# A differential attention in which each pair of score tiles waits for its own rotated tiles

## The chip, the cores and the metric

The kernel runs on one core of one Trainium2 chip. The metric is the device time of one execution in microseconds. Five engines work side by side: TensorE (PE) multiplies, VectorE (DVE), ScalarE (ACT) and GpSimd (POOL) do the rest, SyncE (SP) issues most transfers. They meet at semaphores.

## The reference

Two blocks are computed on 512 tokens of width 1024, in float32. The first has a recurrent unit, a sparse attention and a mixture of 32 experts. The second has two layers, and only these are touched. A layer projects its input to three attentions and their gates:

```
(na_q, na_k, na_v, df_q, df_k, df_v, m_cq, m_ckv, m_kr, gate_pre) = split(x @ w_in[l])
na_out  = neighbourhood_attention(...)          # 8 heads of 64
# differential attention, 4 heads, two score matrices each:
q1, q2, k1, k2 = rope(...)                      # first 16 of 64 dims rotated
o   = softmax(q1 k1) v - lam * softmax(q2 k2) v
df_out = rms_norm(o, subln_g) * (1 - lam_init)  # over the 128 values of a head
mla_out = latent_attention(m_cq, m_ckv, m_kr, ...)
merged = sum_i sigmoid(gate_i) * (out_i @ w_branch[i]);  x = layer_norm(a*x + merged @ w_out)
# then a gated feed-forward of width 2816 and a second layer_norm
```

## The kernel before

Everything is kept transposed: 128 features on the partitions, 512 tokens in the free dimension, so a "tile" is 128x512. Weights come in slots of 16 chunks (128x128 each, 1 MB a slot) through a ring of five slots. A product of full accuracy is made of three fast ones (`tile3`, L437 to L439): high part times high part, high times low, low times high. So each slot is split: ACT copies its high part (`weights_hi`, L486) into one of three high slots, and POOL subtracts (`weights_lo`, L496). A slot's high place comes free when PE begins the next slot (`said`, semaphore `w_used`). The order in which slots come is written in `stream_plan`, and every engine walks the same order by hand.

Products land in two double-buffered pairs of PSUM banks: A (banks 0 and 1, emptied by ACT) and B (banks 2 and 3, emptied by DVE). `claim` on PE waits until the bank before the last one is free; `take` waits until it is full.

Per layer, PE goes through these stages, and the change touches all but the first:

1. First attention (`units_pe`), with the tiles of its gate woven in.
2. `out_tile` of `na_o`: eight tiles of four chunk products each, of the attention's output. They read `o_hi` and `o_lo`, which DVE makes in `heads_split` (L1270, L1271) after the last head.
3. `values(df_v)` (L972 to L974): the values of the second attention, 96 matmuls, in three passes over two slots.
4. Eight tiles `df_qk` (four of queries, one per head, then four of keys). ACT copies each to `raw`, PE multiplies it by a permutation (`turn`, L993, bank B), DVE rotates it (`rope`, L1275 to L1278) and signals `roped`.
5. The pairs: 16 of them, (head, query block). In step i PE makes the two score tiles of pair i (L1012; banks 4 and 5 for even pairs, 2 and 3, which are B's, for odd ones), a part of a gate tile (`woven`, L727 to L729), the transposes of pair i-2 (L1021), and after a head's fourth pair its product with the values (L1028). DVE takes two maxima (L1308), ACT two exponents (L1164), DVE scales and joins them (`pair`, L1298 to L1301).
6. Latent projections: five tiles (`cq`, `mckv`) and a narrow one (`kr`), and between them the norm of the four heads. For head m: ACT squares it into `sqb` (L472), DVE copies it to `acc` (L542), PE sums over the partitions by four products with a column of ones (`squares_pe`, L448), DVE and ACT take the inverse root (L552 to L565), PE spreads it over the partitions (`spread_pe`, L457) after the next tile, DVE copies the spread from PSUM to `acc` (L568) and scales the head (L1319). The next head's copy L542 stands behind that in DVE's order, since both use `acc`.
7. Tiles of the second attention's output, which read its own high and low parts, mixed with more gates; then the third attention.

Of the kernel before, what the change touches and what calls it, by code (L numbers as in the profile page):

```python
# [8 lines left out]
P = 128  # L9
SEQ = 512  # L10
D = 1024
DC = D // P
NQB = SEQ // P
# [68 lines left out]
def stream_plan():  # L82

    gates = [(f"mg{m}", CHUNKS) for m in range(MG_SLOTS)]
    first = [("xr", RC * DC), ("rg", 2 * RC), ("ckv", KVC * DC), ("qi", 4 * DC), ("ki", DC),
             ("wi", 1), ("gr", RC * DC)] + gates + [("q", HEADS * DC),
             ("uk", HEADS * KVC), ("uv", 4 * 2 * KVC), ("rnn_out", DC * RC), ("att_out", DC * DC),
             ("out", DC * DC), ("router", 3)]
    layer = [("na_v", 4 * DC), ("na_qk", 8 * DC), ("na_g", DC * DC), ("na_o", 4 * DC),
             ("df_v", 4 * DC), ("df_qk", 8 * DC), ("df_g", DC * DC), ("cq", MQC * DC), ("mckv", KVC * DC), ("kr", DC)]  # L90
    layer += [(f"df_o{n}", 4) if kind == "o" else (f"ml_g{n}", DC) for step in MIXED for kind, n in step]
    layer += [("qb", HEADS * MQC), ("kvb_k", 4 * KVC), ("kvb_v", 4 * KVC), ("ml_g", (DC - EARLY) * DC), ("ml_o", 4 * DC),
             ("out2", DC * DC), ("ffn_in", 2 * FFC * DC), ("ffn_out", DC * FFC)]

    blocks = {"uv": 16, "na_v": 16, "df_v": 16, "qb": 16, "kvb_v": 8, "ml_g": 16, "rg": 16, "ckv": 16, "gr": 16, "mg0": 16,
              "rnn_out": 16, "att_out": 16, "router": 16}

    def place(parts, at):
        found = {}
        for name, n in parts:  # L100
            if name in blocks:
                at += -at % blocks[name]
            found[name] = at
            at += n
        return found, at + -at % CHUNKS

    one, end = place(first, 0)
    two, size = place(layer, 0)
    return one, end, two, size
# [49 lines left out]
def build(nc, xT, crow, wmod, wrest, wfirst, wlayers, consts, vectors, brow, frow, lamv, rpb, w13, w2, out):  # L159
# [16 lines left out]
    with ExitStack() as ctx:  # L176
# [4 lines left out]
        def sem(name):  # L181
            return ctx.enter_context(nc.semaphore(name))
# [185 lines left out]
            "h1_turned", "h1_kept", "row_in", "h2_rdy", "v_mean", "v_squared", "v_scale", "v_rdy", "v_rest_rdy", "v_turned", "x_rdy"))  # L368
        lam_in, lam_sum, lam_exp = (sem(n) for n in ("lam_in", "lam_sum", "lam_exp"))
        rp_in, near_rdy, roped, keys_rdy = (sem(n) for n in ("rp_in", "near_rdy", "roped", "keys_rdy"))  # L370
        pair_exp, pair_norm, pair_turned, pair_pt = (sem(n) for n in ("pair_exp", "pair_norm", "pair_turned", "pair_pt"))
        pair_sc, pair_mx, o_rdy, merged_rdy = (sem(n) for n in ("pair_sc", "pair_mx", "o_rdy", "merged_rdy"))
        dev_rdy, dev_sq, dev_sq_in, norm_sums, norm_products, out_rdy = (sem(n) for n in (
# [360 lines left out]
        def units_pe(pe, units, ready, Pb=Pb, fill=None):  # L734

            U = len(units)
            for i in range(U + 3):
                if i < U:
                    u = units[i]
                    k = cnt["pv"] + i  # L740
                    ready(i)
                    if k >= 2:
                        pe.wait_ge(exp_done, k - 1)
                    ins = pe.matmul(ps[:, 4 + k % 2, 0:u["nk"] * P], u["q"], u["k"], start=True, stop=True)  # L744
                    ins.then_inc(sc_rdy, 1)
                if fill is not None:
                    fill(i)
                if 2 <= i < U + 2:
                    u = units[i - 2]
                    k = cnt["pv"] + i - 2  # L750
                    if u["summed"]:
                        pe.wait_ge(exp_done, k + 1)
                    else:
                        cnt["scaled"] += 1
                        pe.wait_ge(p_norm, cnt["scaled"])
                    if k >= 2:
                        pe.wait_ge(pt_rdy, k - 1)
                    for j in range(u["nk"]):
                        ins = pe.transpose(ps[:, 6 + k % 2, j * P:(j + 1) * P], Pb[:, k % 3, j * P:(j + 1) * P], ident)  # L759
                    ins.then_inc(turned, 1)  # L760
                if i >= 3 and "sum" in units[i - 3]:
                    pe.wait_ge(pt_rdy, cnt["pv"] + i - 2)
                    units[i - 3]["sum"](pe)
            cnt["pv"] += U
# [182 lines left out]
        def layer_pe(pe, l):  # L947
# [33 lines left out]
                tile3(pe, A.claim(pe), base["na_qk"] + m * DC, *xa, DC).then_inc(A.full, 1)  # L981
            assert B.made == B2 + l * B_LAYER, (B.made, B2)
            units_pe(pe, na_units(), lambda i: pe.wait_ge(A.free, A.made) if i == 0 else None, P2, woven(pe, base["na_g"], xa, DC, 3, 4))
            for m in range(DC):
                out_tile(base["na_o"] + 4 * m, 0, m)


            values(base["df_v"])

            def turn(perm, m, n=P):  # L990

# [5 lines left out]
                if m >= 1:  # L997
                    turn(K("perm_d"), A.made - 1)
            turn(K("perm_d"), A.made)
            pe.wait_ge(B.free, B.made)  # L1000
            pe.wait_ge(roped, l * 16 + 8)
            U = len(pairs)
            fill = woven(pe, base["df_g"], xa, DC, 1, 2)
            for i in range(U + 3):
                if i < U:
                    h, qb = pairs[i]
                    k = l * U + i
                    if k >= 2:
                        pe.wait_ge(pair_exp, 2 * (k - 1))
                    for a in range(2):  # L1010
                        r = 64 * a
                        pe.matmul(ps[:, pair_banks[k % 2][a], :], qk2[r:r + 64, h, qb * P:(qb + 1) * P], qk2[r:r + 64, 4 + h, :],  # L1012
                                  start=True, stop=True).then_inc(pair_sc, 1)
                fill(i)
                if 2 <= i < U + 2:
                    k = l * U + i - 2
                    pe.wait_ge(pair_norm, k + 1)
                    if k >= 2:
                        pe.wait_ge(pair_pt, k - 1)
                    for j in range(NQB):  # L1020
                        ins = pe.transpose(ps[:, 6 + k % 2, j * P:(j + 1) * P], P2[:, 2 * (k % 2), j * P:(j + 1) * P], ident)  # L1021
                    ins.then_inc(pair_turned, 1)
                if i >= 3 and pairs[i - 3][1] == NQB - 1:
                    h = pairs[i - 3][0]
                    pe.wait_ge(pair_pt, l * U + i - 2)
                    b = A.claim(pe)
                    for j in range(NQB):
                        ins = pe.matmul(b, v2[:, j, h * P:(h + 1) * P], PT2s[h % 2][:, j, :], start=(j == 0), stop=(j == NQB - 1))  # L1028
                    ins.then_inc(A.full, 1)

            for m in range(MQC + KVC):
                tile3(pe, A.claim(pe), base["cq"] + m * DC, *xa, DC).then_inc(A.full, 1)
                if m >= 1:
                    spread_pe(pe)
                if m < 4:
                    squares_pe(pe, 1)
            tile3(pe, A.claim(pe)[0:MLA_QK, :], base["kr"], *xa, DC, MLA_QK).then_inc(A.full, 1)
            kr_copied = A.made

# [63 lines left out]
        def layer_act(act, l):  # L1103
# [17 lines left out]

            def df_gates(i):

                if 2 <= i <= 16 and i % 2 == 0:
                    gate(df_gate[:, i // 2 - 1, :], 1, i // 2 - 1)

            def ml_gates(i):
# [14 lines left out]
                copy(qk2[:, m, :])  # L1142

            units_act(act, na_units(), None, P2, PT2s, gates=na_gates, between=na_weights, pv_before=B2 + l * B_LAYER)
            for m in (0, 4):
                weights_hi(act, base["na_o"] + 4 * m)

            for s_ in range(NQB):
                weights_hi(act, end1 + l * size2 + two["df_v"] + (CHUNKS if s_ == NQB - 1 else 0))
                copy(v2[:, s_, :])  # L1150
            for m in range(8):
                weights_hi(act, end1 + l * size2 + two["df_qk"] + m * DC)
                if m >= 2:
                    act.wait_ge(roped, l * 16 + m - 1)
                copy(raw[:, m % 2, :])
# [20 lines left out]
                if i % 4 == 2:  # L1176
                    weights_hi(act, base["df_g"] + (i // 4) * CHUNKS)
            act.wait_ge(A.free, A.took)
            squares(act, o2[:, 0:1, :], 1)
            for h in range(4):  # L1180
                if h + 1 < 4:
                    squares(act, o2[:, h + 1:h + 2, :], 1)
                weights_hi(act, end1 + l * size2 + two["cq"] + h * DC)
                copy(cq[:, h, :] if h < MQC else ckv2[:, h - MQC, :])
                root(act)
# [55 lines left out]
        def layer_dve(dve, l):  # L1241
# [70 lines left out]
            pair(U - 1)  # L1312
            a += 4 + DC
            for h in range(4):
                if h >= 1:
                    dve.wait_ge(o_rdy, 4 * l + h)
                sum_squares(dve, 1)
                inverse_var(dve, P, EPS)
                STT(out=o2[:, h, :], in0=o2[:, h, :], scalar=subg[:, l:l + 1], in1=rstd, op0=ALU.mult, op1=ALU.mult).then_inc(o_rdy, 1)  # L1319
            dve.wait_ge(A.free, a)  # L1320
            a += MQC + KVC + 1 + EARLY
            dve.wait_ge(o_rdy, 4 * (l + 1))
# [1283 lines left out]
```

## Time and profile before

| | |
|---|---|
| median of 3 runs | 3422.34 us (3411.9, 3422.34, 3423.8) |
| profiled execution | 3408.22 us, of which span 3406.1 us |
| PE busy in the span | 3062.2 us, 90% |
| DVE, ACT, POOL busy | 1547.6, 988.7, 941.6 us |
| chain that ended last, by engine | PE 74%, DMA 12%, DVE 9%, ACT 3% |
| mean granted clock of PE | 0.969 of 2.4 GHz |
| stages 2 to 6, layer 0 | 1395 to 1640 us of the span |
| stages 2 to 6, layer 1 | 2477 to 2728 us |

The profile is one execution. A line of the trace has the start, the busy time, the engine, the line of the kernel, what is written and read, and in brackets how long the engine had been idle and what ended that. A granted clock of 1.00 is 2.4 GHz, one of 0.50 is 1.2 GHz; a window between shows a mixture.

### The profile page before, as it was taken

The numbers are of one execution on the slowest core, as the hardware profiler recorded it, in microseconds if no ns is written. First come the engines' busy times: TensorE is split into PE (matmuls) and PEld (weight loads), VectorE is DVE, ScalarE is ACT, GpSimd is POOL, SyncE is SP. The second block draws the span as 40 slices with busy tenths as digits, with TensorE's granted clock in tenths as the row PEclk, the third lists the DMA queues.
The fourth block names the chain that finished last, engine by engine and source line by source line (L and its number), as shares of the span: only waits on it lengthen the run. The fifth ranks groups of instructions, "written<-read, shape, count | busy, mean of one in ns | idle before, by whom it ended". The sixth has DMA issues, their size and how long they took to land.

```text
span 3406.1 us, 32962 instructions
## 1 busy us (share of the span) xinstructions
PE 3062.2 (90%) x13112; PEld 2096.4 (62%) x13112; DVE 1547.6 (45%) x2578; ACT 988.7 (29%) x1398; POOL 941.6 (28%) x346
## 2 busy tenths in 40 slices
PE   3999998787777679999998899999999899889998
PEld 2777656632222256766655788877776665578886
DVE  7598866421111135455557622231636365752233
ACT  3553232200000043234253322223424334232222
POOL 2243102200000044322121444445432221244432
PEclk9999999899999989999999899999999899989999
DMA  5236212499999941211211222222121121112221
GB/s 225 85 124 237 98 50 87 167 400 422 422 422 422 384 145 62 75 62 50 77 48 39 73 99 99 99 87 94 49 87 50 50 83 42 50 63 98 99 99 50
DMA packets 71228, 465.80 MB, mean 137 GB/s; under 512 B 8784, under 2 KB 9072, under 8 KB 18992
## 3 DMA queue, kind: packets, MB, share of 16 engines
q1 hardware_dynamic: 60192, 436.31, 33.4%
q0 software_dynamic: 5200, 17.07, 1.4%
q10 hardware_dynamic: 5696, 10.49, 0.8%
q8 instruction: 95, 1.56, 0.2%
q14 instruction: 45, 0.37, 0.0%
HBM read 451.24 MB, written 12.60 MB: 136 GB/s over the span
## 4 chain that ended last, share of the span: by engine, by line
PE 74%; DMA 12%; DVE 9%; ACT 3%; issue 1%; POOL 0%; SPq 0%; ACTq 0%; DVEq 0%; POOLq 0%
PE ps L437 15%; PE ps L439 14%; PE ps L438 14%; DMA mring<-w 10%; PE ps L744 3%; PE ps L727 3%; PE ps L729 2%; PE ps L728 2%; PE ps L426 2%; PE ps L2248 2%; PE ps L907 1%; PE ps L759 1%; PE ps L1012 1%; PE ps L2323 1%; PE ps L1028 1%
## 5 line engine op out<-in xcount | busy, mean ns | idle before, releaser
L496 POOL TENSOR_TENSOR w_lo<-wring,w_hi 128x2048 fp32r<-128x2048 f32 (+1 forms) x198 | 812.6, 4111 | 1776.6 <-ACT w_hi L486 1776.5
L437 PE MATMUL ps<-x_hi,w_hi 128*128 128x512 f32 (+1 forms) x1480 | 593.0, 401 | 18.2 <-ACT ps L1585 7.8
L439 PE MATMUL ps<-x_hi,w_lo 128*128 128x512 f32 (+1 forms) x1480 | 582.7, 394 | 0.0
L486 ACT ACTIVATE w_hi<-wring 128x2048 fp32r<-128x2048 f32 x176 | 336.0, 1911 | 322.0 <-PE ps L437 284.7
L438 PE MATMUL ps<-xf_lo,w_hi 128*128 128x512 f32 x1080 | 422.2, 391 | 0.0
L437 PEld LDWEIGHTS ps<-x_hi,w_hi 128*128 128x128 f32 (+1 forms) x1480 | 281.8, 190 | 91.3 <-issue 8.4
L439 PEld LDWEIGHTS ps<-x_hi,w_lo 128*128 128x128 f32 (+1 forms) x1480 | 281.3, 190 | 60.7
L2322 PE MATMUL ps<-mring,xT__95 128*64 128x512 f32 x512 | 239.9, 600 | 58.3 <-DMA mring<-w 54.5
L2323 PE MATMUL ps<-mring,xT__95 128*64 128x512 f32 x512 | 240.2, 601 | 0.0
L438 PEld LDWEIGHTS ps<-xf_lo,w_hi 128*128 128x128 f32 x1080 | 204.1, 189 | 41.6
L1360 DVE TENSOR_TENSOR g_f<-ps,g_f 128x512 f32<-128x512 f32 x44 | 30.4, 692 | 366.7 <-PE ps L439 350.4
L2322 PEld LDWEIGHTS ps<-mring,xT__95 128*64 128x64 f32 x512 | 63.5, 136 | 185.7 <-DMA mring<-w 123.8
L438 PE MATMUL ps<-xa_lo,w_hi 128*128 128x512 f32 (+1 forms) x400 | 160.6, 401 | 0.0
L727 PE MATMUL ps<-x_hi,w_hi 128*128 128x512 f32 x336 | 159.2, 474 | 0.0
L2341 PE MATMUL ps<-mring,hidT 128*64 128x512 f32 x512 | 117.7, 602 | 42.4 <-DVE hidT L2080 42.4
L1692 ACT ACTIVATE sil<-ps 64x512 f32<-64x512 f32 x32 | 19.0, 595 | 471.1 <-PE ps L2323 471.1
L2075 DVE TENSOR_TENSOR hid<-ps,sil 64x512 f32<-64x512 f32 x32 | 21.8, 683 | 293.5 <-ACT sil L1692 293.5
L1476 POOL DMA_INDIRECT xs<-u_rows,ids x16 | 15.2, 951 | 461.9 <-PE ps L2311 405.5
L437 PE MATMUL ps<-g_hi,w_hi 128*128 128x512 f32 x352 | 137.7, 391 | 0.0
L439 PE MATMUL ps<-g_hi,w_lo 128*128 128x512 f32 x352 | 137.0, 389 | 0.0
L438 PE MATMUL ps<-g_lo,w_hi 128*128 128x512 f32 x352 | 137.0, 389 | 0.0
L729 PE MATMUL ps<-x_hi,w_lo 128*128 128x512 f32 x336 | 133.1, 396 | 0.0
(518 smaller groups left out, 5488.2 us busy)
## 6 DMA issues: line engine op xcount, KB each, us to landing
mring<-w SPq DMA_DIRECT2D x192, 1024.0 KB, 28.3
wring<-wlayers SPq DMA_DIRECT2D x148, 1024.0 KB, 4.8
wring<-wfirst SPq DMA_DIRECT2D x44, 1024.0 KB, 4.8
mods<-wrest SPq DMA_DIRECT2D x16, 1024.0 KB, 4.7
wmodS<-wmod SPq DMA_DIRECT2D x4, 2048.0 KB, 18.4
y_rows<-ysb ACTq DMA_DIRECT2D x64, 128.0 KB, 6.7
rp<-rpb POOLq DMA_DIRECT2D x16, 192.0 KB, 2.6
hT<-xT SPq DMA_DIRECT2D x1, 2048.0 KB, 18.2
```

The source lines that it names most:

```text
L426: ins = pe.matmul(bank, w[:, 0:m], rhs[:, k, :], start=(k == 0), stop=(k == nk - 1))
L437: said(pe.matmul(bank, wh[:, 0:m], hi[:, k, :], start=(k == 0), stop=False))
L438: pe.matmul(bank, wh[:, 0:m], lo[:, k, :], start=False, stop=False)
L439: ins = pe.matmul(bank, wl[:, 0:m], hi[:, k, :], start=False, stop=(k == nk - 1))
L486: act.activation(w_hi[:, q % HI_SLOTS, :], wring[:, home(g), :], ACT.Copy).then_inc(hi_rdy, 1)
L496: ins = pool.tensor_tensor(w_lo[:, home(slot), o:o + n], wring[:, home(slot), o:o + n], w_hi[:, q % HI_SLOTS, o:o + n].bitcast(F32), ALU.s ...
L727: said(pe.matmul(state["bank"], wh, x[0][:, k, :], start=(k == 0), stop=False))
L729: ins = pe.matmul(state["bank"], wl, x[0][:, k, :], start=False, stop=(k == DC - 1))
L744: ins = pe.matmul(ps[:, 4 + k % 2, 0:u["nk"] * P], u["q"], u["k"], start=True, stop=True)
L2322: pe.matmul(ps[MOE_ROWS:P, 2 + a, :], x, w[:, 0:SEQ], start=(k == 0), stop=(k == DC - 1))
L2323: ins = pe.matmul(ps[0:MOE_ROWS, 2 + a, :], x, w[:, SEQ:D], start=(k == 0), stop=(k == DC - 1))
L2341: ins = pe.matmul(ps[n * MOE_ROWS:(n + 1) * MOE_ROWS, 5 + a, :], hidT[:, a, k, :], w[:, n * SEQ:(n + 1) * SEQ], start=(k == 0), stop=(k == 3))
```

## The change

Four edits, in both layers of the second block:

- In the weights' order, on PE and on ACT, `df_v` comes ahead of `na_o`. DVE's order stays as it was.
- PE no longer waits for all eight rotated tiles before the pairs. The first pair of head h waits for `roped` up to key tile h (tiles 0 to 4+h), and pair 1 for the last turned tile to be out of bank B.
- The gate products are woven in quarters of a tile (6 matmuls): one each in steps 0, 1, 16 and 17, two in steps 2 to 15. Before it was a half (12 matmuls) in steps 1 to 16. ACT takes the last gate in step 17 and not in step 16.
- In the heads' norm PE sums straight from `sqb`, where ACT puts the squares, and DVE scales the head by the spread in PSUM. L542 and L568 are gone for the heads.

```diff
-    layer = [..., ("na_g", DC * DC), ("na_o", 4 * DC),
-             ("df_v", 4 * DC), ("df_qk", 8 * DC), ...
+    layer = [..., ("na_g", DC * DC), ("df_v", 4 * DC),
+             ("na_o", 4 * DC), ("df_qk", 8 * DC), ...
...
+            values(base["df_v"])
             for m in range(DC):
                 out_tile(base["na_o"] + 4 * m, 0, m)
-            values(base["df_v"])
...
-            pe.wait_ge(B.free, B.made)
-            pe.wait_ge(roped, l * 16 + 8)
             U = len(pairs)
-            fill = woven(pe, base["df_g"], xa, DC, 1, 2)
+            fill = woven(pe, base["df_g"], xa, DC, 0, 4)
+            pieces = [1, 1] + [2] * (U - 2) + [1, 1]
             for i in range(U + 3):
                 if i < U:
                     h, qb = pairs[i]
                     k = l * U + i
+                    if qb == 0:
+                        pe.wait_ge(roped, l * 16 + 4 + h + 1)
+                    if i == 1:
+                        pe.wait_ge(B.free, B.made)
...
-                fill(i)
+                for n in range(sum(pieces[:i]), sum(pieces[:i + 1])):
+                    fill(n)
...
                 if m < 4:
-                    squares_pe(pe, 1)
+                    pe.wait_ge(head_squared, 4 * l + m + 1)
+                    b = B.claim(pe)
+                    for s in range(NQB):
+                        ins = pe.matmul(b[:, s:s + 1], sqb[:, m % 2, s * P:(s + 1) * P], ones[:, 0:1], ...)
+                    ins.then_inc(B.full, 1)
...
-                if 2 <= i <= 16 and i % 2 == 0:
+                if 2 <= i <= 14 and i % 2 == 0 or i == 17:
                     gate(df_gate[:, i // 2 - 1, :], 1, i // 2 - 1)
...
-            for m in (0, 4):
-                weights_hi(act, base["na_o"] + 4 * m)
             for s_ in range(NQB):
                 weights_hi(act, ... two["df_v"] ...)
                 copy(v2[:, s_, :])
+            for m in (0, 4):
+                weights_hi(act, base["na_o"] + 4 * m)
...
-            squares(act, o2[:, 0:1, :], 1)
+            act.wait_ge(sq_added, cnt["sq_a"])
+            def head_square(h):
+                act.activation(sqb[:, h % 2, :], o2[:, h, :], ACT.Square).then_inc(head_squared, 1)
+            head_square(0)
             for h in range(4):
                 if h + 1 < 4:
-                    squares(act, o2[:, h + 1:h + 2, :], 1)
+                    head_square(h + 1)
...
             for h in range(4):
-                if h >= 1:
-                    dve.wait_ge(o_rdy, 4 * l + h)
-                sum_squares(dve, 1)
-                inverse_var(dve, P, EPS)
-                STT(out=o2[:, h, :], in0=o2[:, h, :], scalar=subg[:, l:l + 1], in1=rstd, ...)
+                inverse_root(dve, P, EPS)
+                STT(out=o2[:, h, :], in0=o2[:, h, :], scalar=subg[:, l:l + 1], in1=B.take(dve), ...)
+                free_bank_b(dve)
```

## Rows read from the trace of the kernel before

**Rows 1.** Page, part 1: busy time, share of the span, instructions.

```profile
PE 3062.2 (90%) x13112; PEld 2096.4 (62%) x13112; DVE 1547.6 (45%) x2578; ACT 988.7 (29%) x1398; POOL 941.6 (28%) x346
```

**Rows 2.** Windows, both layers: length, busy PE PEld DVE ACT POOL, granted clock, DMA.

```profile
1395.00:1640.00 245.00, 229.40 (x968) 166.49 (x967) 107.67 (x214) 80.85 (x134) 72.74 (x27) 0.97 0.19 65
2477.00:2728.00 251.00, 235.65 (x962) 170.67 (x962) 107.16 (x213) 80.52 (x133) 72.48 (x27) 0.94 0.18 63
```

**Rows 3.** Waits of PE, layer 0: waiting line, releaser: total us, times, longest.

```profile
PE ps L448 <- DVE acc L542: 8.0, 4, 2.0
PE ps L1012 <- DVE qk L1278: 2.7, 1, 2.7
PE ps L437 <- DVE o_lo L1271: 2.1, 1, 2.1
```

**Rows 4.** Timeline, first attention's end, both layers: start, us, instruction, [idle before].

```profile
1397.77 0.47 PE L437 MATMUL ps<-o_hi,w_hi 128*128 128x512 f32 x1 [2.13 <-DVE o_lo L1271]
...
1401.68 0.39 PE L437 MATMUL ps<-o_hi,w_hi 128*128 128x512 f32 x1
...
2479.14 0.75 PE L437 MATMUL ps<-o_hi,w_hi 128*128 128x512 f32 x1 [2.13 <-DVE o_lo L1271]
...
2483.56 0.39 PE L437 MATMUL ps<-o_hi,w_hi 128*128 128x512 f32 x1
```

**Rows 5.** Timeline at the start of the pairs, layer 0.

```profile
1491.76 2.03 PE L993 MATMUL ps<-raw,cs 128*128 128x512 f32 x4
1496.50 3.47 PE L1012 MATMUL ps<-qk 64*128 64x512 f32 x8 [2.71 <-DVE qk L1278]
...
1498.58 0.69 DVE L1308 TENSOR_REDUCE small<-ps 128x1 f32<-128x512 f32 x1 [2.23 <-PE ps L1012]
...
1500.28 0.69 ACT L1164 ACTIVATE P<-ps,small 128x512 f32<-128x512 f32 x1
...
1503.90 0.50 PE L727 MATMUL ps<-x_hi,w_hi 128*128 128x512 f32 x1
...
1506.78 0.60 PE L1021 MATMUL ps<-cs,P 128*128 128x128 f32 x4
1507.31 1.13 PE L1012 MATMUL ps<-qk 64*128 64x512 f32 x4
1508.37 0.50 PE L727 MATMUL ps<-x_hi,w_hi 128*128 128x512 f32 x1
```

**Rows 6.** Timeline at the last pair, layer 0.

```profile
1571.29 1.13 PE L1012 MATMUL ps<-qk 64*128 64x512 f32 x4
...
1580.89 0.66 PE L1021 MATMUL ps<-cs,P 128*128 128x128 f32 x4 [1.80 <-DVE P L1301]
```

**Rows 7.** Timeline of PE in the latent projections, layers 0 and 1.

```profile
1585.37 0.79 PE L437 MATMUL ps<-x_hi,w_hi 128*128 128x512 f32 x1
...
1601.42 1.05 PE L457 MATMUL ps<-cs,small 128*128 128x128 f32 x8
1604.51 1.13 PE L448 MATMUL ps<-cs,acc 128*128 128x1 f32 x8 [2.03 <-DVE acc L542]
...
1634.10 0.48 PE L437 MATMUL ps<-x_hi,w_hi 128*96 128x512 f32 x1
...
2670.34 0.80 PE L437 MATMUL ps<-x_hi,w_hi 128*128 128x512 f32 x1
...
2722.35 0.48 PE L437 MATMUL ps<-x_hi,w_hi 128*96 128x512 f32 x1
```

**Rows 8.** Windows around two of the falls of the clock, columns as in 2.

```profile
1604.00:1610.00 6.00, 5.49 (x21) 4.60 (x22) 1.43 (x7) 2.52 (x3) 1.24 (x1) 0.72 0.46 147
...
2700.00:2708.00 8.00, 7.33 (x22) 6.08 (x23) 1.58 (x8) 0.21 (x1) 0.00 (x0) 0.57 0.00 0
```

**Rows 9.** Page, part 5: splitting a weight slot into high and low parts.

```profile
L496 POOL TENSOR_TENSOR w_lo<-wring,w_hi 128x2048 fp32r<-128x2048 f32 (+1 forms) x198 | 812.6, 4111 | 1776.6 <-ACT w_hi L486 1776.5
...
L486 ACT ACTIVATE w_hi<-wring 128x2048 fp32r<-128x2048 f32 x176 | 336.0, 1911 | 322.0 <-PE ps L437 284.7
```

More of the change, by code:

```diff
@@ L88, in stream_plan @@
              ("out", DC * DC), ("router", 3)]
-    layer = [("na_v", 4 * DC), ("na_qk", 8 * DC), ("na_g", DC * DC), ("na_o", 4 * DC),
-             ("df_v", 4 * DC), ("df_qk", 8 * DC), ("df_g", DC * DC), ("cq", MQC * DC), ("mckv", KVC * DC), ("kr", DC)]
+    layer = [("na_v", 4 * DC), ("na_qk", 8 * DC), ("na_g", DC * DC), ("df_v", 4 * DC),
+             ("na_o", 4 * DC), ("df_qk", 8 * DC), ("df_g", DC * DC), ("cq", MQC * DC), ("mckv", KVC * DC), ("kr", DC)]
     layer += [(f"df_o{n}", 4) if kind == "o" else (f"ml_g{n}", DC) for step in MIXED for kind, n in step]
@@ L370, in build @@
         rp_in, near_rdy, roped, keys_rdy = (sem(n) for n in ("rp_in", "near_rdy", "roped", "keys_rdy"))
+        head_squared = sem("head_squared")
         pair_exp, pair_norm, pair_turned, pair_pt = (sem(n) for n in ("pair_exp", "pair_norm", "pair_turned", "pair_pt"))
@@ L1035, in layer_pe @@
                 if m < 4:
-                    squares_pe(pe, 1)
+                    pe.wait_ge(head_squared, 4 * l + m + 1)
+                    b = B.claim(pe)
+                    for s in range(NQB):
+                        ins = pe.matmul(b[:, s:s + 1], sqb[:, m % 2, s * P:(s + 1) * P], ones[:, 0:1], start=True, stop=True)
+                    ins.then_inc(B.full, 1)
             tile3(pe, A.claim(pe)[0:MLA_QK, :], base["kr"], *xa, DC, MLA_QK).then_inc(A.full, 1)
@@ L1314, in layer_dve @@
             for h in range(4):
-                if h >= 1:
-                    dve.wait_ge(o_rdy, 4 * l + h)
-                sum_squares(dve, 1)
-                inverse_var(dve, P, EPS)
-                STT(out=o2[:, h, :], in0=o2[:, h, :], scalar=subg[:, l:l + 1], in1=rstd, op0=ALU.mult, op1=ALU.mult).then_inc(o_rdy, 1)
+                inverse_root(dve, P, EPS)
+                STT(out=o2[:, h, :], in0=o2[:, h, :], scalar=subg[:, l:l + 1], in1=B.take(dve), op0=ALU.mult, op1=ALU.mult).then_inc(o_rdy, 1)
+                free_bank_b(dve)
             dve.wait_ge(A.free, a)
```

## The prediction

> **What bounds the kernel now.** I read the page first: PE is busy for 90% of the span [rows 1], so a change pays only where PE stands still, or where it runs at half clock. Then the windows over the stretch from the end of the first attention to the second attention's output, once per layer. The same work takes some 245 us in layer 0 and 251 us in layer 1; PE is busy for about 94% of both, and its mean clock is 0.97 and 0.94 [rows 2]. Hence about 15.5 us idle in each, and about 245 x 0.03 = 7 and 251 x 0.06 = 15 us of clock lost. DMA stands at 0.19 and POOL under a third, so neither weights nor their splitting set the pace.
>
> Third the waits of PE in layer 0, to see what ends the idle time [rows 3]. Three entries belong to the change: 8.0 us in four waits for DVE's copy of the squares, 2.7 us for the last rotated tile, 2.1 us for the first low part. Layer 1 has the same ones within 0.05 us.
>
> Last the clock, by small windows. Eleven windows hold all of its falls in the two stretches. A fall costs the whole of 6.0 x (1 - 0.72) = 1.7 us where it is single, and 8.0 x (1 - 0.57) = 3.4 us where it is double [rows 8]. In layer 0 one fall stands at the pairs' start and three in the latent projections, 6.8 us. In layer 1 one at the first attention's end, one at the pairs' start, a double one at the pairs' end, and in the projections a double one and three single ones: 15.3 us. Each begins behind one of the waits above, or while one lasts.
>
> **Edit 1, values first.** In layer 0 the first output tile begins after 2.13 us idle, and its four chunks then follow DVE's low parts: from 1397.77 to 1401.68 is 3.91 us [rows 4], where twelve matmuls at an undisturbed pitch take 2.75 us (rows 5 have it: 12 in 1503.90 to 1506.78 is 2.88, of which some 0.1 is the change of kind). With the values first, DVE splits the heads while PE works for over 20 us on operands that are there, so 2.13 + 1.2 = 3.3 us go. Layer 1: 2.13 + (2483.56 - 2479.14 - 2.75) = 3.8 us, its clock loss included [rows 4]. Sum 7.1 us.
>
> What is moved with it are the splits of slots. The values read their two slots in three passes and hold the first until 2.7 us before their end, so two of three high places stay taken. The output's first slot goes into the third place at once. Its second slot can be split only from then on: 1.9 us on ACT and 4.1 us on POOL [rows 9], 6.0 us, and it is needed 2.7 + 16 x 0.68 = 13.6 us later. The splits cost nothing as long as this cover of 7.6 us holds; the third rival takes it away. POOL's split now meets `heads_split` on DVE; both have more than 15 us to spare.
>
> **Edit 2, the pairs' start.** Before: turns from 1491.76, scores at 1496.50 after 2.71 us idle and partly at half clock, first transposes at 1506.78 [rows 5]. After: the turns end at about 1493.7, head 0 needs only key tile 4, done long before, so pair 0's scores run until 1494.8 (1.06 each, from 1507.31 to 1508.37) and a quarter of gate (1.5) until 1496.2. By then DVE has read the last turned tile, about 0.8 us ahead of the 1496.50 at which the rotation was known to be ready, so pair 1 goes on to 1497.3 and the second quarter to 1498.8. Step 2 needs pair 0's two exponents. DVE's maxima still stand behind its last rotation, so they begin at about 1496.4 instead of 1498.58; the second exponent began 1.70 us after that and takes 0.9 with its sum [rows 5], so PE is let on at 1499.0: 0.2 us of idle is left of 2.71. Scores and half a tile of gates bring the transposes to 1503.0. Pair 0's weights are ready at about 1496.4 + 2 x 1.70 + 1.6 = 1501.4. From there both kernels have the same work behind them. The gain is 1506.78 - 1503.0 = 3.8 us, of which 1.7 are clock. Twice, 7.6 us. Bounds: 2.1 us each if the clock falls anyway.
>
> **Edit 3, quarters.** The same 192 matmuls; slot limits fall at the same steps (5, 9, 13). Four more changes of kind at about 0.1 us. At the end I count no gain: pair 15's transposes start 1580.89 - 1571.29 = 9.6 us after its scores start, released by DVE [rows 6]. The new order has in that time 1.06 of scores, 2.88 + 1.5 + 1.5 of gates and two transposes of 0.53, 8.0 us; so PE still waits for DVE and ends at the same place, only in smaller waits. Bound above: the 1.80 of idle, twice. Bound below: if DVE were earlier, the last quarter could hold the transposes up by 1.5 us, twice.
>
> **Edit 4, squares from ACT's place.** The chain spread, copy L568, scale L1319, copy L542, squares is cut to spread, squares. In layer 0 the five tiles with their norms take 1634.10 - 1585.37 = 48.7 us, in layer 1 2722.35 - 2670.34 = 52.0 [rows 7]. Less the idle 8.0 [rows 3] and the clock loss of 5.1 and 8.5 (above) both give 35.5 us: the two layers agree on what the work takes alone. Nothing new should hold it: head m's squares lie ready a tile ahead (ACT makes them before the copy of tile m), the inverse root needs about 1.5 us and the spread comes 5.5 us later, and DVE frees the bank of the spread with the scaling, under 1 us. The gain is 13.2 + 16.5 = 29.7 us; without the clock 16.1.
>
> **Sum.** 7.1 + 7.6 + 29.7 = 44.4 us if no fall of the clock takes the place of a removed one. I charge 4 us, two or three single falls over the eight joints of spread and squares, where 2.1 us of small matmuls (1.05 each, [rows 7]) now follow each other. That gives 40 us: 3368 us for the profiled execution of 3408.22. The median of the runs shown is 14.1 us above that execution; what it holds more is not in this trace, and I leave it in. **3422.3 - 40 = 3382 us.**
>
> The spread multiplies by the identity, as a transpose does, and no row separates how such matmuls count for the clock. The Trainium skill, page TensorE: Matmul & The Clock Gate, Part 4: PE-mode transpose, states that transposes do not count as work in this way; here, with transposes in every step of the pairs, no window of them shows a low clock behind the first step, though gates fill these. By that rule the joints would stay slack for the clock, and the first rival would be likelier.
>
> **Rivals.** First, the clock falls all the same. For it: the falls come beside stretches with little matmul work, and spread plus squares are such. Against: the joint shrinks from 1.05 + 2.03 + 1.05 = 4.1 us [rows 7] to 2.1, and even at 4.1 one of eight stayed at full clock. Gain by idle alone: 2 x (2.13 + 1.2) + 2 x 2.1 + 16.1 = 27 us, so 3395 us. Chance 0.13.
>
> Second, a wait takes the place of the one removed at the pairs' start or in the norms, so that the change does only part of what it says. DVE still does its eight rotations before any maximum, and ACT's `root` stands behind a copy and, for heads 2 and 3, a split. If the pairs' start gave nothing and each of the later three joints kept 1.5 us, the gain would be 44.4 - 7.6 - 9 - 4 = 24 us, 3398 us; with the clock as in the first rival some 10, 3412 us. Against: the margins above, 4 us at each spread. Chance 0.10, of which 0.06 within 0.5%.
>
> Third, the other side: splits come late. If a slot of `na_o` or `df_qk` is not split when PE arrives, PE stands with all behind it. Cover is 7.6 us; a whole slot's delay beyond it costs 6.0 us and a fall of the clock, 1.7 [rows 8], and up to four slots per layer could be hit: 2 x 4 x 7.7 = 62 us against 40, 3444 us. It decides from 7.6 us lateness on. Against: POOL is busy a third of the stretch and DMA a fifth [rows 2]. Chance 0.03, and about half of it would be slower by over 0.5%.
>
> Fourth, more than I say: the pairs' end gives its 1.80 twice and the double fall there is gone (3.4): 44.4 + 7 = 51 us, 3371 us. Chance 0.10. The forecast itself has 0.64.
>
> **Range.** 0.5%, 17 us, is about what a measurement of this kernel can tell from no change; the three runs shown lie 12 us apart. Low end: 3371 less 9 of such scatter, 3362. High end: 3395 and 6 of scatter, 3401; that leaves out the worst of the second rival and the third. Faster by over 0.5%: 0.64 + 0.13 + 0.10 + 0.04 = 0.91; within: 0.06 + 0.01, 0.07; slower 0.02.
>
> **What would show it.** Right: the values' first matmul follows the last L885 without idle time, and the first output tile has an even pitch; scores of pair 0 right after the turns, a wait for ACT of under 0.5 us in step 2, the first transposes about 11.2 us after the turns' start and not 15.0; no wait before the squares' sums, L542 and L568 gone from the stage, and first `cq` tile to `kr` in about 35.5 to 39 us. Wrong: waits of PE on the exponents in steps 2 to 4, a clock of 0.50 at more than half of the norm's joints, or waits on the first matmul of a slot.

## The result, and the profile after

| | before | after |
|---|---|---|
| median | 3421.46 us (4 runs, 3411.9 to 3423.8) | 3365.55 us (4 runs, 3363.76 to 3368.4) |
| ratio | | 0.9839, 95% interval 0.9825 to 0.9853 |
| profiled execution | 3408.22 us | 3363.76 us |
| mean clock in it | 0.969 | 0.973 |

The kernel became 56 us faster, 1.6%. The forecast was 40 us and 3382 us, with a range from 3362 to 3401. The two profiled executions lie 44.5 us apart, and the sum before its charge for the clock was 44.4 us. That they agree so well is luck: the two stretches that the change touches became 48.8 us shorter, and the rest of the span, which it doesn't touch, came out 4.7 us longer in the changed kernel's profile (2911.1 and 2915.8 us). The experiments ask where the other 11 us of the medians come from, and whether each term is what it was said to be.

First the page of the changed kernel, busy time by engine. PE has 17 us less of busy time than in [rows 1] for the same 13112 matmuls: matmuls at half clock are longer ones.

```profile
PE 3045.0 (91%) x13112; PEld 2082.9 (62%) x13112; DVE 1536.4 (46%) x2562; ACT 988.9 (29%) x1398; POOL 942.7 (28%) x346
```

Then the windows of the two stretches, from the first attention's last product to the second attention's output (length, busy PE, PEld, DVE, ACT, POOL, clock, DMA share, GB/s). They answer to [rows 2]. They were 245 and 251 us long there; now both are 223.7 (223.1 from mark to mark, as the stretches are measured below), with the clock at 1.00 and 2.3 us idle in place of 15.5.

```profile
1397.80:1621.50 223.70, 221.40 (x967) 161.86 (x966) 101.92 (x206) 80.66 (x133) 72.78 (x27) 1.00 0.20 71
2460.80:2684.50 223.70, 221.40 (x967) 161.81 (x965) 101.93 (x206) 80.56 (x133) 72.77 (x27) 1.00 0.20 71
```

The waits of PE in the first stretch answer to [rows 3]. All three entries are gone. What stands instead is small: two waits for the weights of the last two pairs and one for the last transposed tile, as before.

```profile
PE ps L1024 <- DVE P L1311: 1.6, 2, 1.2
PE ps L1031 <- ACT PT2b L1177: 0.7, 1, 0.7
```

At the end of the first attention [rows 4] the values start right behind the last product, with no idle time in brackets, and the output's chunks run at an even 0.68 us from the first on:

```profile
1396.01 2.40 PE L886 MATMUL ps<-PT2b,v 128*64 128x128 f32 x20
1398.34 0.50 PE L973 MATMUL ps<-w_hi,x_hi 128*128 128x512 f32 x1
...
1420.53 0.39 PE L438 MATMUL ps<-o_hi,w_hi 128*128 128x512 f32 x1
...
1421.20 0.39 PE L438 MATMUL ps<-o_hi,w_hi 128*128 128x512 f32 x1
...
1421.88 0.39 PE L438 MATMUL ps<-o_hi,w_hi 128*128 128x512 f32 x1
```

At the start of the pairs [rows 5] the turns begin at 1491.25, scores of pairs 0, 1 and 2 follow at 1493.21, 1495.85 and 1498.50 with a quarter of gate between them, none of them after a recorded wait. The first transposes come 11.17 us after the turns' start; the forecast was 11.2, before it was 15.02:

```profile
1491.25 2.03 PE L992 MATMUL ps<-raw,cs 128*128 128x512 f32 x4
1493.21 1.13 PE L1014 MATMUL ps<-qk 64*128 64x512 f32 x4
...
1495.85 1.13 PE L1014 MATMUL ps<-qk 64*128 64x512 f32 x4
...
1498.50 1.13 PE L1014 MATMUL ps<-qk 64*128 64x512 f32 x4
...
1502.42 0.60 PE L1024 MATMUL ps<-cs,P 128*128 128x128 f32 x4
```

At the last pair [rows 6] the 1.80 us have split in two, 1.18 and 0.42: together 1.6 us, which is what the prediction's 9.6 us less 8.0 leave. The last transposes start 1576.53 - 1566.93 = 9.6 us after the scores, as before. The product with the values still waits its 0.69, and POOL's split (5.64 us) still runs beside DVE's scaling of pair 14 (1.65 us here, 0.75 undisturbed):

```profile
1566.93 1.13 PE L1014 MATMUL ps<-qk 64*128 64x512 f32 x4
...
1569.51 5.64 POOL L497 TENSOR_TENSOR w_lo<-wring,w_hi 128x512 fp32r<-128x512 f32 x4 [15.70 <-ACT w_hi L487]
...
1572.36 1.65 DVE L1311 SCALAR_TENSOR_TENSOR P<-P,small 128x512 f32<-128x512 f32 x1
...
1574.07 0.66 PE L1024 MATMUL ps<-cs,P 128*128 128x128 f32 x4 [1.18 <-DVE P L1311]
...
1576.53 0.65 PE L1024 MATMUL ps<-cs,P 128*128 128x128 f32 x4 [0.42 <-DVE P L1311]
...
1577.87 3.70 PE L1031 MATMUL ps<-PT2b,v 128*128 128x512 f32 x8 [0.69 <-ACT PT2b L1177]
```

In the latent projections [rows 7] the sums of squares (L1042) follow the spread (L458) at once. From the first latent tile to `kr` it is 1615.87 - 1581.01 = 34.9 us, in layer 1 too. The forecast was 35.5; before they took 48.7 and 52.0:

```profile
1581.01 0.79 PE L438 MATMUL ps<-x_hi,w_hi 128*128 128x512 f32 x1
...
1593.26 1.05 PE L458 MATMUL ps<-cs,small 128*128 128x128 f32 x8
1594.15 0.95 PE L1042 MATMUL ps<-cs,sqb 128*128 128x1 f32 x8
...
1615.87 0.48 PE L438 MATMUL ps<-x_hi,w_hi 128*96 128x512 f32 x1
```

### The profile page after: what moved, and what is told of

It is laid out like the page before. It is cut to its first block, busy times and chain, and to the rows that moved or that the text cites. A ratio compares the mean times of both kernels' runs of the same rounds, so it can differ in the third digit from the quotient of the medians.

```text
span 3361.9 us, 32946 instructions
## 1 busy us (share of the span) xinstructions
PE 3045.0 (91%) x13112; PEld 2082.9 (62%) x13112; DVE 1536.4 (46%) x2562; ACT 988.9 (29%) x1398; POOL 942.7 (28%) x346
## 4 chain that ended last, share of the span: by engine, by line
PE 75%; DMA 12%; DVE 8%; ACT 2%; issue 1%; POOL 0%; SPq 0%; ACTq 0%; DVEq 0%; POOLq 0%
PE ps L438 15%; PE ps L439 14%; PE ps L440 14%; DMA mring<-w 10%; PE ps L745 3%; PE ps L728 3%; PE ps L730 2%; PE ps L729 2%; PE ps L427 2%; PE ps L2256 2%; PE ps L908 2%; PE ps L760 1%; PE ps L2330 1%; PE ps L1014 1%; PE ps L973 1%
```

## The experiments

Each kernel was timed in five rounds against the kernel before. All ratios below are to the kernel before on the same chip. I cut each profile into stages at marks, in each layer: the first attention's end, the start of the first and of the last pair's scores, the first latent tile, `kr`, and the first tile of the second attention's output. The latent stage is the part from the first latent tile to `kr`; a stretch goes from the first mark to the last. A fall of the clock is a piece of time in which the granted clock is 0.50 and not 1.00.

**Each edit alone.** The four kernels are the kernel before with one of the hunks of the change shown above.

> The kernel before with edit 1 alone (df_v ahead of na_o in the weights' order, on PE and on ACT). My account: 3.3 us of layer 0 and 3.8 us of layer 1 go, 7 us, ratio 0.998; no idle time between the first attention and the next matmul, even pitch in the first output tile. Rival, clock: as many falls as before turn up elsewhere and the gain is the idle time alone, 4 us to 7 us. Rival, late splits: PE waits for a slot in na_o or df_qk, ratio 1.000 or more.

> The kernel before with edit 2 alone (each head's first pair waits for its own rotated tiles; gate halves from step 1 as before). My account: pair 0's scores directly behind the turns, pair 1 held for about 0.9 us by the last turned tile, first transposes about 11.8 us after the start of the turns where before had 15.0 (11.2 in the changed kernel): 3.2 us per layer, 6 us, ratio 0.998. Rival, a wait in place of the wait: PE stops at step 2 for the exponents of pair 0 for 2 us or more and the ratio is 0.9995 or more.

> The kernel before with edit 3 alone (quarters of gate tiles in steps 0 to 17, pairs start only when all eight tiles are rotated). My account: nothing gained at either end, since DVE's chain from the last scores ends the stage; idle at the last two transposes 1.18 and 0.42 us in place of 1.80; ratio 1.000 within 0.0007. Rival: the smaller waits keep the clock up at the pairs' end, up to 3.4 us, ratio 0.999.

> The kernel before with edit 4 alone (PE sums squares from sqb, DVE scales from PSUM). My account: first latent tile to kr in about 35.5 us where before had 48.7 and 52.0, 16 us of idle and 13.6 us of clock, so 30 us and ratio 0.991. Rival, the clock still falls at the joints: 16 us, ratio 0.995. If the median of before holds more falls of the clock than its profiled execution did, the gain is above 30 us, up to 40.

| kernel | median us | ratio, 95% interval | gain of the medians |
|---|---|---|---|
| before (29 runs) | 3420.44 | | |
| values_only | 3411.45 | 0.9973 (0.9964 to 0.9982) | 9.0 |
| pairs_only | 3412.28 | 0.9979 (0.9969 to 0.9989) | 8.2 |
| quarters_only | 3415.31 | 0.9986 (0.9976 to 0.9997) | 5.1 |
| squares_only | 3384.97 | 0.9896 (0.9880 to 0.9913) | 35.5 |

The four add up to 57.8 us, and together they gave 55.9 in the first comparison. Each gain is uncertain by 3 to 6 us, so no edit is seen to take from another, but a few us of that could not be seen. In values_only the way from the first attention's end to the first scores is 97.6 and 97.5 us, where the fourteen stretches of the other profiles that keep this part have 100.8 to 102.0, 101.2 in the mean. That is 3.7 us per layer, 7.3 of the 9.0. In pairs_only the first transposes come 11.87 us behind the turns' start in both layers, where the expectation had 11.8, and PE waits 0.8 us there, ahead of pair 1's scores. In squares_only the latent stage is 34.9 us in both layers. In quarters_only the way from the last scores to the first latent tile is 14.1 us in both layers; see below.

**The kernel before again.**

> The kernel before, unchanged. It asks why the medians moved by 56 us and the two profiled executions by 44.5 us. Theory: the falls of TensorE's clock behind the waits are drawn anew in each execution, and the first profiled one had few; then executions of this kernel scatter by 10 us and more, the mean clock is lower where the time is longer (0.001 of mean clock is 3.4 us lost), and this profile shows another set of falls in the two stretches than 6.8 and 15.3 us. Rival: the 14 us lie in the transfers of the experts or another stage; then the falls are the same set and the clock does not go with the time. Ratio 1.000.

Ratio 0.9999 (0.9990 to 1.0008). The profile caught an execution of 3423.83 us at a mean clock of 0.962. Its windows over the two stretches, in the form of [rows 2]:

```profile
1403.20:1654.70 251.50, 236.12 (x966) 170.96 (x965) 107.35 (x214) 80.63 (x133) 72.47 (x27) 0.94 0.18 63
2496.80:2746.30 249.50, 233.92 (x966) 170.16 (x965) 107.34 (x214) 80.64 (x133) 72.70 (x27) 0.95 0.18 64
```

The stretches take 250.9 and 248.9 us between the marks, 499.8 together, where the first profile had 244.1 and 250.9, 495.0. By the windows PE is idle for 251.50 - 236.12 = 15.4 and 15.6 us in them, as in [rows 2]. What differs is which waits a fall follows. Of the other 11 us between the two executions 8.2 lie ahead of the first stretch and 5.4 between the stretches, and 2.7 come off behind the second. The clock goes the same way in each part: the loss (length times one minus the granted clock) is 13.7 us larger ahead, 6.8 larger between and 3.4 smaller behind, 101.7 us outside the stretches in place of 84.6. Over 70 executions of this kernel the time goes with the mean clock: 14 at 0.962 take 3423.6 us in the mean, 14 at 0.964 take 3420.2, 6 at 0.966 take 3415.9, and 2 at 0.968 take 3408.7. A straight line through all 70 has 2.3 us for each 0.001, where the expectation had 3.4, all of the lost clock; so part of the loss costs no time. So the first profiled execution, 3408.22 us at 0.969, was one with few falls; only one of those 70 was as short. The rival, a stage that lengthens without the clock, is not what the parts show.

**The wait filled with useless work.** Before each sum of squares:

```diff
                 if m < 4:
+                    for n in range(9):
+                        pe.matmul(ps[:, 4, :], x_hi[:, n % DC, 0:P], x_hi[:, n % DC, :], start=True, stop=True)
                     squares_pe(pe, 1)
```

> The kernel before, with nine fast matmuls of 512 columns into an unused bank ahead of each of the four sums of squares: 2.1 us of work that fills the wait of 2.03 us, its result is used by nobody. It separates idle time from clock. If the falls of the clock are a cost of their own, set off by the waits, the projections show no fall and take about 43.6 us (35.5 + 8) in place of 48.7 and 52.0, 13.6 us less by the first profile: ratio 0.996 or lower. If the idle time is all, the ratio is 1.000 or a little above.

Median 3406.65 us, ratio 0.9955 (0.9941 to 0.9969). The kernel does 36 matmuls more per layer, removes no wait and is 14 us faster. The first latent tile, a spread, the sums of squares behind it and the end of the stage, in the timeline of PE of layer 0:

```profile
1596.78 0.80 PE L437 MATMUL ps<-x_hi,w_hi 128*128 128x512 f32 x1
...
1611.28 1.05 PE L457 MATMUL ps<-cs,small 128*128 128x128 f32 x8
...
1614.36 1.05 PE L448 MATMUL ps<-cs,acc 128*128 128x1 f32 x8
...
1641.04 0.48 PE L437 MATMUL ps<-x_hi,w_hi 128*96 128x512 f32 x1
```

The sums (L448) still come 3.08 us behind the spread, as in [rows 7]. But the stage has the clock at 1.00 in both layers, and takes 44.3 us (1641.04 - 1596.78) and 44.2. So the falls behind these waits are a cost of their own. Without them the waits cost 44.3 - 34.9 = 9.4 us per layer; with them the stage takes 51.2 in the mean of twelve stretches, so 6.9 us per layer are clock.

**The same at the pairs' end.** In step 17, ahead of the wait for the last pair's weights:

```diff
+                if i == U + 1:
+                    for n in range(8):
+                        pe.matmul(ps[:, 4, :], x_hi[:, n % DC, 0:P], x_hi[:, n % DC, :], start=True, stop=True)
                 if 2 <= i < U + 2:
```

> The kernel before, with eight fast matmuls of 512 columns into an unused bank in step 17 of the pairs, where PE waits 1.80 us for the last pair's weights; nobody uses the result. It asks where edit 3's gain comes from, as no work was taken away by it. If the falls of the clock at the pairs' end are set off by that wait, then from the last scores to the first latent tile it is 14.1 to 14.2 us in both layers, where executions of before have 14.1, 15.8 or 17.1, and the ratio is 0.9988. If they come from something else, 15.8 and 17.1 stay and the ratio is 1.000.

Ratio 0.9986 (0.9975 to 0.9997), median 3414.19 against 3421.47 us: the result of quarters_only, with nothing changed but the idle time covered. In the timeline of layer 1 the eight useless matmuls take the place of the wait, and from the last scores to the first latent tile it is 2673.80 - 2659.70 = 14.1 us:

```profile
2659.70 1.13 PE L1012 MATMUL ps<-qk 64*128 64x512 f32 x4
...
2667.26 2.09 PE L1017 MATMUL ps<-x_hi 128*128 128x512 f32 x8
2669.32 0.66 PE L1024 MATMUL ps<-cs,P 128*128 128x128 f32 x4
2670.67 3.70 PE L1031 MATMUL ps<-PT2b,v 128*128 128x512 f32 x8 [0.69 <-ACT PT2b L1174]
2673.80 0.79 PE L437 MATMUL ps<-x_hi,w_hi 128*128 128x512 f32 x1
```

In the same place of the kernel before, the transposes follow the wait, and the product behind them takes 6.74 us in place of 3.70, for the clock has fallen:

```profile
2662.82 0.66 PE L1021 MATMUL ps<-cs,P 128*128 128x128 f32 x4 [1.80 <-DVE P L1301]
2664.16 6.74 PE L1028 MATMUL ps<-PT2b,v 128*128 128x512 f32 x8 [0.69 <-ACT PT2b L1171]
```

Over the profiles this stretch reads 14.1 us in all eight cases where the wait is cut in two or filled (quarters_only, busy_end, the changed kernel in two profiles). In the fourteen where it is whole it is 14.1 twice, else 15.5 to 17.1, 16.1 in the mean. That is 2.0 us per layer for edit 3, 4 of its 5.1. The quarters have a small price: in quarters_only the way from the first to the last scores is 75.2 and 75.1 us, where the two profiles of before have 74.8 to 74.9 with a fall in it, and 73.2 without.

**Half of edit 4.** PE and ACT as in the whole edit, but DVE keeps the copy of the spread, which is in `inverse_var`. Against the kernel before, DVE's part is:

```diff
             for h in range(4):
                 if h >= 1:
                     dve.wait_ge(o_rdy, 4 * l + h)
-                sum_squares(dve, 1)
                 inverse_var(dve, P, EPS)
                 STT(out=o2[:, h, :], ..., in1=rstd, ...)
```

> The kernel before with half of edit 4: PE sums from sqb, so the copy L542 is gone, but DVE still copies the spread from PSUM to acc and scales from there. My account: what held PE was that L542 stood behind the scaling in DVE's order; with L542 gone the copy of the spread is under 1 us of DVE work with 4 us of cover, so the gain is that of the whole edit, ratio 0.991. Rival: the copy L568 is half of the chain; then PE still waits about 0.7 us per head and the ratio is 0.993 to 0.994.

Ratio 0.9906 (0.9891 to 0.9921), whole edit 0.9896 (0.9880 to 0.9913): no difference that the intervals show, and the stage takes 34.9 us in both. The copy L569 and the scaling run beside PE's next tile, and nobody waits for them:

```profile
1608.98 1.05 PE L458 MATMUL ps<-cs,small 128*128 128x128 f32 x8
...
1609.87 0.95 PE L1040 MATMUL ps<-cs,sqb 128*128 128x1 f32 x8
1610.07 0.69 DVE L569 COPY acc<-ps 128x512 f32<-128x512 f32 x1 [4.37 <-PE ps L458]
...
1610.80 0.75 DVE L1327 SCALAR_TENSOR_TENSOR o<-o,small,acc 128x512 f32<-128x512 f32 x1
```

So what pays is that PE no longer reads what DVE copies behind the scaling of the head before.

**The split that collides with the last pairs.** The changed kernel, with ACT's split of step 14 left to the call of step 18, and then at step 17:

```diff
-                if i % 4 == 2:
+                if i % 4 == 2 and i != 14:              # split_later
+                if i % 4 == 2 and i != 14 or i == 17:   # split_at_17
                     weights_hi(act, base["df_g"] + ...)
```

> The changed kernel, with ACT's split of the weight slot in step 14 of the pairs left to the call in step 18, so that POOL's four pieces do not run beside DVE's last two pairs. Ratio is against the kernel before. If POOL's pieces hold DVE up there, the scaling of pair 14 takes 0.5 and 0.75 us where it took 1.5 and 1.7, the waits of 1.18 and 0.42 us before the last transposes go, and the kernel is 2 to 3 us faster than the changed one per two layers, ratio about 0.983. Rival: the slot is then late for the latent projections and PE waits there; the ratio is no better than that of the changed kernel.

> The changed kernel with the weight split of step 14 moved to step 17, behind ACT's last gate. Ratio is against the kernel before. From the last scores to the first latent tile 12.2 us in place of 14.1, as with the split in step 18, but the split is ready earlier, so that POOL's two splits end before PE needs head 0's spread: latent stage 34.9 us and not 36.1. Then 3.8 us in all against the changed kernel, ratio 0.9828. Rival: POOL still holds DVE's small products of head 0 past the end of the second latent tile, PE waits 1 us per layer, ratio 0.984.

> The changed kernel, unchanged, on the same chip as the two others. Ratio 0.9839. It asks whether its two stretches are free of falls of the clock in a second profile too: 223.1 us each if so. If falls are drawn anew here as well, some 1.7 us more in one of them.

| kernel | median us | ratio, 95% interval | last scores to first latent tile | latent stage |
|---|---|---|---|---|
| split_later | 3366.98 | 0.9843 (0.9829 to 0.9856) | 12.2 | 36.1 |
| split_at_17 | 3365.76 | 0.9834 (0.9821 to 0.9848) | 12.3 | 34.9 |
| after_again | 3368.37 | 0.9848 (0.9835 to 0.9861) | 14.1 | 34.9 |

With the split gone from beside DVE, both waits of 1.18 and 0.42 us go. In split_later a new one comes: POOL works off two slots in a row, and a DVE product of four columns, 0.17 us with no subtraction beside it, takes 4.47 us beside it; PE then waits 0.91 us for the spread. So each side of the expectation was half right: the two waits go, and the late slot costs a new one.

```profile
1591.68 4.61 POOL L497 TENSOR_TENSOR w_lo<-wring,w_hi 128x2048 fp32r<-128x2048 f32 x1
...
1591.84 4.47 DVE L563 TENSOR_TENSOR small<-small 128x4 f32<-128x4 f32 x1 [0.98 <-ACT small L532]
1596.34 0.16 DVE L564 TENSOR_TENSOR small<-small 128x4 f32<-128x4 f32 x1
...
1596.96 1.16 PE L458 MATMUL ps<-cs,small 128*128 128x128 f32 x8 [0.91 <-DVE small L566]
```

The product starts 0.16 us behind POOL's subtraction of 128x2048 and ends with it: 1591.84 + 4.47 = 1596.31, and 1591.68 + 4.61 = 1596.29. In split_at_17 POOL begins 3.7 us earlier; the product starts later in its subtraction and again ends with it, at 1592.62 and 1592.60. There it takes 0.65 us and delays nobody:

```profile
1588.00 4.60 POOL L497 TENSOR_TENSOR w_lo<-wring,w_hi 128x2048 fp32r<-128x2048 f32 x1
...
1591.97 0.65 DVE L563 TENSOR_TENSOR small<-small 128x4 f32<-128x4 f32 x1 [0.98 <-ACT small L532]
...
1596.02 1.05 PE L458 MATMUL ps<-cs,small 128*128 128x128 f32 x8
```

In split_at_17 both stretches take 221.3 us instead of 223.1, so 3.6 us in all; in split_later 222.3. Between the medians of split_at_17 and after_again there are 2.6 us, with intervals that overlap: it is the best version by its profile, and the times neither confirm nor contradict it. The second profile of the changed kernel has 223.1 us and no fall of the clock in both stretches, like the first.

## Why the prediction was right, and where its sizes were off

**The result as a whole.** The forecast's account of what holds PE, and of what each edit takes away, came true, and most of the gain is where it was put. That the time lies in the range is in part luck: 3365.55 us is 16.5 below the forecast and 3.6 above the low end, and that end was drawn for the fourth rival with 9 us of scatter, not for the reasons that follow.

**Edit 1, 7.1 us.** Right: 3.7 us per layer in the marks, 9.0 us (6 to 12) in the medians. The slots were never late, so the third rival had no part: no wait on a weight slot appears in the stretches.

**Edit 2, 7.6 us.** Right: 8.2 us alone (4 to 11); in the changed kernel's profile edits 1 and 2 together shortened the two ways from the first attention to the last scores by 14.8 us, where the sum had 14.7; the first transposes stand where they were put, and the 0.2 us of idle in step 2 did not even show.

**Edit 3, nothing at the end.** The place was right: waits of 1.18 and 0.42 us, the stage ends with DVE's chain. The statement "I count no gain" was wrong by the clock: 5.1 us (1 to 8) alone, 2.0 us per layer in the marks. Behind one wait of 1.80 us the clock fell in twelve of fourteen cases; behind the two short ones it did in none of six. The fourth rival had half of this: the fall goes, the wait itself doesn't. It took the double fall of layer 1 for the only one, when a single or a double one was the rule.

**Edit 4, 29.7 us.** The chain, the 8 us of idle per layer and the 35.5 us that remain were right; 34.9 came out. The size was low for two reasons. 1.3 us are the step from 35.5 to 34.9, twice. The rest is that "the clock loss of 5.1 and 8.5" was read from one execution: the latent stage lasts 48.7 to 53.6 us over the twelve cases without edit 4 and without useless work in these waits, 51.2 in the mean where the first profile has 50.4, so 16.3 us per layer on the way to 34.9: 32.6 us. The medians say 35.5 (30 to 41).

**The charge of 4 us for the clock at the joints.** Wrong, it is zero. A layer has three joints of spread and squares and not four, since the first squares have no spread before them and the last spread has no squares behind it: six in an execution where the prediction counted eight. In the six profiles with edit 4 that makes 36, and no latent stage of them holds a fall. The first rival, that the clock falls all the same, is out. In busy_wait, too, where the spreads and sums stay and only the wait between them is filled, no latent stage holds one. So it takes the wait for the clock to fall here; the 2.1 us of small matmuls alone don't do it. What a longer run of them would do no run shows. The Trainium skill, page TensorE: Matmul & The Clock Gate, Part 4: PE-mode transpose, states that transposes do not count as work of PE in the same way. If the spreads counted like them, the first rival would have been the likelier one; at these joints no fall bears that out.

**The second rival,** a wait in place of the wait, did not come either: 2.3 us of idle are left per layer, all at the pairs' end.

**"I leave it in", the 14.1 us between profile and median.** With the charge of 4 us and the pairs' end, this is what made the size too small. Part of those 14 us was not a fixed addition but more falls of the same kind, and the change removes those that lie in its stretches: 4.8 us of the 15.6 between the two profiles of before. The two stretches went from 495.0 or 499.8 us to 446.2, so 48.8 or 53.6 us. Idle time and clock account for both: 31.0 us idle became 4.6, and the clock's loss of 22.2 or 27.3 us became nothing, 48.6 and 53.7 us. Against the medians' 55.9 (and 53.1 in the last comparison) that leaves a few us. The scatter of the rest, 2911 to 2922 us outside the stretches, is wide enough to cover them, but no run shows where they lie. The changed kernel itself lies within 1.8 us of its profiled execution.

## What to carry to other kernels

A wait on TensorE is to be priced with what the clock does behind it, and that price is a mean over executions: read a second profile, or the mean clock of all runs, before taking the falls of one trace as the kernel's. Where a wait can't be removed, cutting it in two by moving work between (or even filling it with useless matmuls) can keep the clock: here a wait of 1.80 us, cut into 1.18 and 0.42, gave 2.0 us per layer. When a small result is passed through another engine's scratch tile, look for what stands before that copy in its order: one buffer shared by the next head's input and this head's factor had put the scaling of one head and the copies on both sides of it into TensorE's path before the next head's sums.

## What the runs showed of the hardware

- Behind waits of 1.8 to 2.7 us the granted clock fell to 0.50 in most cases, at a cost of 1.7 us of TensorE's time or 3.4; 72 useless matmuls in eight of these waits made the kernel 14 us faster.
- The whole kernel's time moves with these falls: 3408 to 3425 us in 70 executions, 2.3 us for each 0.001 of mean clock.
- A DVE product of two 128x4 operands took 4.47 us beside a POOL subtraction of 128x2048, and 0.65 us when it started later in one. It ended with that subtraction in both profiles and both layers, so what POOL's operation can hold up is not set by the size of the DVE instruction. The Trainium skill says why on its page SBUF — State Buffer, section Who interferes with whom: a DVE instruction with two inputs in SBUF contends with a GpSimd instruction that reads SBUF; both profiles agree with it. The same product (L563) with no subtraction beside it took 0.17 us in the changed kernel.
